# Scaling the prompt's attention probabilities in the product that transposes them

## The reference, cut to what matters

```
s = einsum('bqgjd,bsgd->bgjqs', q, k) + bias
p = masked_softmax(s, mask)          # exp(s - max) / sum
o = einsum('bgjqs,bsgd->bqgjd', p, v)
mix_n = g[0] * o_c + g[1] * o_s + g[2] * o_w      # g: sigmoid gates, one for each token, branch and head
```

## Time and profile before

| | us |
|---|---|
| median of 3 runs | 1063.69 (1063.34 to 1071.04) |
| the profiled execution | 1065.43 |
| its span, first to last instruction | 1063.7 |

### The profile page before, as it was taken

The page is one execution under the profiler, slowest core; times in us unless marked ns, Lnnn a source line. Parts: engine busy times, 40 slices in busy tenths (PEclk is TensorE's granted clock), DMA queues, the critical chain, the costliest instruction groups (busy, mean ns, idle before and its releaser), DMA issues.

```text
span 1063.7 us, 19859 instructions
## 1 busy us (share of the span) xinstructions
PE 921.4 (87%) x7903; PEld 824.2 (77%) x7903; DVE 517.3 (49%) x1116; ACT 374.3 (35%) x742; POOL 99.3 (9%) x164
## 2 busy tenths in 40 slices
PE   5865898899988758698888976999999999999994
PEld 5764687677877647355557966999999999999992
DVE  3610224642233564666664237667676676422325
ACT  4220234463532010155563136343443434222215
POOL 1001121334344000200000000000000000000000
PEclk9976898999999555558899998999999999999997
DMA  8256677757735000220003211232222222222212
GB/s 284 79 114 142 192 234 263 239 191 222 214 108 200 1 6 1 94 118 1 1 1 124 80 40 40 80 99 80 86 95 79 99 81 77 90 80 87 87 32 85
DMA packets 53135, 112.44 MB, mean 106 GB/s; under 512 B 6945, under 2 KB 30274, under 8 KB 52594
## 3 DMA queue, kind: packets, MB, share of 16 engines
q1 hardware_dynamic: 44616, 89.06, 25.3%
q0 software_dynamic: 6528, 17.83, 5.3%
q10 hardware_dynamic: 1898, 4.27, 2.5%
HBM read 102.92 MB, written 12.38 MB: 108 GB/s over the span
## 4 chain that ended last, share of the span: by engine, by line
PE 76%; DVE 9%; DMA 5%; ACT 4%; issue 3%; SPq 2%; ACTq 0%; POOLq 0%; POOL 0%; DVEq 0%
PE q L1667 28%; PE q L1665 26%; DMA arena<-in_pool 5%; PE q L2112 2%; PE q L2130 2%; PE q L2140 2%; PE q L1729 1%; PE q L2000 1%; PE q L2173 1%; PE q L2174 1%; PE q L2054 1%; PE q L1717 1%; PE q L1783 1%; PE q L1963 1%; DVE xt L1529 1%
## 5 line engine op out<-in xcount | busy, mean ns | idle before, releaser
L468 DVE TENSOR_TENSOR wring_r<-wring,whi_r 128x1024 fp32r<-128x1024 f32 (+1 forms) x101 | 120.5, 1193 | 366.9 <-ACT whi_r L465 366.7
L465 ACT ACTIVATE whi_r<-wring 128x1024 fp32r<-128x1024 f32 (+1 forms) x101 | 104.2, 1033 | 325.0 <-PE q L1667 314.3
L1667 PE MATMUL q<-xt_r,whi_r 128*128 128x288 f32 x552 | 167.7, 304 | 0.0
L1665 PE MATMUL q<-xt_r,whi_r 128*128 128x256 f32 x552 | 158.2, 287 | 0.0
L1665 PE MATMUL q<-arena_r,whi_r 128*128 128x256 f32 x440 | 138.0, 314 | 19.7 <-DVE xt_r L468 11.6
L1667 PE MATMUL q<-arena_r,whi_r 128*128 128x288 f32 x440 | 134.3, 305 | 0.0
L1667 PE MATMUL q<-arena_r,wring_r 128*128 128x288 f32 x440 | 133.5, 303 | 0.0
L1665 PE MATMUL q<-arena_r,wring_r 128*128 128x256 f32 x440 | 126.5, 287 | 0.0
L1665 PE MATMUL q<-mixt_r,whi_r 128*128 128x256 f32 x400 | 113.0, 282 | 10.5 <-DVE xt_r L468 10.5
L1667 PE MATMUL q<-mixt_r,whi_r 128*128 128x288 f32 x400 | 119.2, 298 | 0.0
L1665 PEld LDWEIGHTS q<-xt_r,whi_r 128*128 128x128 f32 x552 | 107.7, 195 | 0.0
(11 more groups left out here) (406 smaller groups left out, 1584.4 us busy)
## 6 DMA issues: line engine op xcount, KB each, us to landing
wring<-in_w_up SPq DMA_DIRECT2D x42, 512.0 KB, 3.3
wring<-in_w_in SPq DMA_DIRECT2D x27, 512.0 KB, 5.2
arena<-in_pool SPq DMA_DIRECT2D x64, 192.0 KB, 3.8
arena<-in_pool POOLq DMA_DIRECT2D x64, 192.0 KB, 4.2
wring<-in_w_down SPq DMA_DIRECT2D x24, 448.0 KB, 3.2
arena<-in_pool POOLq DMA_DIRECT2D x64, 64.0 KB, 2.5
arena<-in_pool SPq DMA_DIRECT2D x64, 64.0 KB, 2.2
wring<-in_w_out SPq DMA_DIRECT2D x8, 512.0 KB, 6.1
```

What stands on the lines that cost most here:

```text
L465: return eng.activation(out, src, ACT.Copy)
L468: return eng.tensor_tensor(out, src, hi.bitcast(F32), ALU.subtract)
L1665: pe.matmul(out[:, 0, 0:HALF], w, x[:, 0:HALF], start=(kk == 0 and n == 0), stop=(end and n == 2))
L1667: mm = pe.matmul(out[:, 1, 0:HALF + NS], w, x[:, HALF:NT], start=(kk == 0 and n == 0), stop=(end and n == 2))
```

## The change

`gated` no longer touches the probabilities. It writes the identity, scaled on each partition by the reciprocal of the sum and by the gate, to a new buffer of 3 slots x 2 heads x 128 columns in `dsc`. L1542 keeps its two instructions for each pair, and each is now 128 columns wide, whatever the width of the pair. `transposed` takes this scaled identity as the moving operand of an ordinary f32 product, where it had the plain identity in a transpose: out[key, query] = sum over p of pb[p, key] * diag[p, query]. The semaphores and their counts stay.

```
+        gated_one = dsc[:, 0:768].rearrange("p (s g c) -> p s g c", s=3, g=NG)
...
                 for g in range(NG):
-                    v, gate = pb[:, slot, g, 0:128 * i + 128], 104 + 24 * i + 8 * k + GQ * g + j
-                    dve.tensor_scalar(v, v, dens[:, 4 + slot, g:g + 1], gcol[:, gate:gate + 1],
+                    gate = 104 + 24 * i + 8 * k + GQ * g + j
+                    dve.tensor_scalar(gated_one[:, slot, g, :], ident, dens[:, 4 + slot, g:g + 1], gcol[:, gate:gate + 1],
                                       ALU.mult, ALU.mult).then_inc(np_p, 1)
...
                     for kk in range(m // 8 + 1):
-                        mm = pe.transpose(bank[4 + g][:, 128 * kk:128 * kk + 128],
-                                          pb[:, m % 3, g, 128 * kk:128 * kk + 128], ident)
+                        mm = pe.matmul(bank[4 + g][:, 128 * kk:128 * kk + 128],
+                                       pb[:, m % 3, g, 128 * kk:128 * kk + 128], gated_one[:, m % 3, g, :],
+                                       start=True, stop=True)
                     mm.then_inc(np_t, 1)
```

## The result

| | us |
|---|---|
| before, median of 4 runs | 1064.23 (1063.34 to 1071.04) |
| changed, median of 4 runs | 1080.40 (1079.21 to 1080.95) |
| changed / before | 1.0136, 95% interval 1.0093 to 1.0179 |
| the changed kernel's profiled execution, and its span | 1080.75, 1079.0 |

Slower by 16.2 us, 1.4%. The forecast was 1075.7 us, in a range of 1068 to 1081. Some kernels further on had one disturbed execution (1121, 1721 and 2194 us), which counts in the median that is given for them but not in the ratio.

A forecast was written before the change was run, and what follows sets the result against it. No engine was full; a loop of waits, TensorE holding the largest share, was taken to bound the prompt attention. 14.7 - 0.5 - 2.2 = +12.0 us on 1063.7 gave 1075.7 us, range 1068 to 1081.

The forecast's parts named there:

- The doubled instruction, 107 ns at the full clock: Line 2140: each product takes two instructions, so 160 more, each 107 ns at full clock, 0.215 us at half.
- Half of it on the path: Loop of two pairs: only every second transpose group stands in it, so about half of a group's extra time counts.
- The stretched chain, 14.7 us: Line 2140's pieces in the chain of waits, stretched: 6.0 at half clock, 6.6 at full, 2.1 in the last groups.
- The tail: Last two transpose groups, with no other work beside them: 0.76 us more each, 1.5 us for both.
- VectorE's pass, -0.5 us: Line 1542, now always 128 wide: 6.4 us less VectorE work, mostly hidden, 0.5 us of it gained.
- The clock, -2.2 us: Prompt attention: with ordinary products TensorE's clock rises a few us earlier than 480 us, taking back 2.2 us.
- the first (the clock pays it back): Prompt attention: products lift the clock early and return most of the cost; 1070 us, or 1067; chance 0.28.
- a hidden second instruction: Line 2140: the second instruction hides behind the weights' load, only VectorE's saving stays; 1063 us; chance 0.05.
- VectorE as the bound: Line 1542: VectorE's 6.4 us come back wholly; 1057 us with a hidden second instruction, about 1070 with doubled; chance 0.05.
- The second (all of it on the path): Line 2140: every stretched group delays a copy and shadows vanish, 20.6 - 0.5 us; 1084 us; chance 0.12.

The follow-up runs named there:

- the control: The kernel before, unchanged, measured and profiled once more: 1066.22 us median, ratio 1.0012, stage 112.3 us.
- short_scale: Against the kernel before: VectorE writes the scaled identity, but line 2140 stays a transpose with the plain identity, so probabilities are never scaled; 1065.22 us, ratio 0.9996.
- plain_product: Against the kernel before: line 2140 as an ordinary f32 product with the plain identity, VectorE still scaling the probabilities in place; 1079.5 us, ratio 1.0124.

## Why the prediction was right

It forecast +12.0 us. The stage grew by 11.8, and three measurements gave +16.2, +14.0 and +10.8. The time of the result, 1080.4 us, is another matter: it stands 0.6 us inside the range's upper end and above the forecast's own 1073 to 1079, because some 4 us came from outside the stage, of which the sum says nothing. That they left it in the range is luck. Step by step:

- *The doubled instruction, 107 ns at the full clock.* Right. L2141 has 320 instructions where L2140 had 160. A group of eight blocks was to take about 1.9 us and takes 1.98. The term was 0.09 us a group too small: the instruction's price was read from other lines and was right (two transposes in its place give 1.89), and the product form adds 0.09. The starts of the single instructions show how: at the full clock the second one of a group starts 0.21 us after the first where it is 0.16 with transposes, and each further one 112 ns after the last instead of 109. No row of before shows that. The lines that the price was read from bear it out in the trace of before: line 2173's two instructions start 0.215 us apart at a clock of 1.00, line 2000's, after the first, 0.213 us at 0.50. Line 2112's, 64 columns wide, start in pairs, 6 or 7 ns within a pair and 103 from one pair to the next, so that 16 of them take 1.03 us to the next group (546.96 to 547.99); it was rightly left aside. At the half clock the instruction costs 213 ns in the trace of after (215 in the sum), and the product form again adds, 0.10 us to the shortest group: the four of two blocks take 1.15 us to the next group (465.74 to 466.89), two transposes 0.62 (465.71 to 466.33 in the trace of before).
- *Half of it on the path.* Right in size, with another picture at the end. 8.2 us were forecast for two pairs, and 8.27 measured. The prediction noted that TensorE's own 4.0 us came near the loop's 4.1. In the trace of after they have met: TensorE has 0.1 us of waiting in two pairs. The kernel with three transposes shows the kink: two pairs go from 7.31 to 8.18 with the second and to 9.70 with the third, +0.9 and then +1.5, nearly the whole 2 x 8 x 0.107 = 1.7. The shadow hid only the first part of the growth here. The prediction's rule, half of the extra time, holds for the loop; tile 3 as a whole grew by 5.7 of 64 x 0.107 = 6.8 us, since its last groups have no such shadow.
- *The stretched chain, 14.7 us.* Split by tile, its pieces come to 1.9, 3.9, 3.6 and 5.3 us. Against the control, and with a third of a us given back for each us less at half, the tiles grew by 2.1, 3.2, 3.4 and 5.7. So the sum is right in its parts too, and not only in total.
- *The tail.* 0.76 us for each of the last two groups was forecast. The last output groups stand 3.76 us apart (570.62 and 574.38 in the chain), 2.92 before (557.19 and 560.10): 0.84, the same 0.09 too little.
- *VectorE's pass, -0.5 us.* Right: 0.5 to 0.7 us by short_scale, with 6 us less work, and 0.1 to 0.3 beside the doubled instruction.
- *The clock, -2.2 us.* An estimate of the author's and the least certain term, about right in size and in part by luck. By the clocks of the four tiles before, TensorE was at half for 17.6 + 18.7 + 7.0 = 43.3 us of the stage, after for 21.1 + 10.8 + 3.1 = 35.0. At 0.33 us each, the 8.3 us are worth 2.7 (3.3 at 0.4). So the price at an equal clock is 11.8 + 2.7 = 14.5 us, where the sum without the clock said 14.2. But the term was argued from one earlier rise, shortly before 480 us. Against the control, tile 1 has only 1.4 us less at half; 2.0 come from tile 0 and 3.9 from tile 2, of which the term says nothing. And the 34 us at half that the prediction counts from the earlier trace rows leave out the stage's first 9 us, up to 456.3, granted half as well; the 0.81 of the earlier trace rows over 115 us makes it 44.

Of the rivals, the first (the clock pays it back) was at work, but with about a fifth of the cost (2.7 of 14.5 us, by the estimate above) and not with most of it. The third and fourth (a hidden second instruction; VectorE as the bound) are excluded by plain_product and short_scale. The second (all of it on the path) is true only of a third transpose in the widest pairs, 6.8 of 6.8 us.

It took the clock to rise sooner with ordinary products in place of the transposes. That was the author's estimate, and the runs bear it out at most in tile 0 (0.57 with products, 0.50 with two transposes). Over the stage two transposes for each block gave 0.86 and 0.84 where the changed kernel had 0.86, and three gave 0.89, the highest of all, with all of these instructions in the transpose form. In tile 3 of that kernel 24 of a pair's 44 instructions are transposes, and the granted clock was 1.00 throughout. In the kernel before, 60 transposes in a row ran at 1.00 for 7.3 us.

## What to carry to other kernels

Ask first what the pass costs where it stands, and then what it becomes where it goes. Here VectorE's pass was waited for 1.1 us in the whole stage, and 6 us less of it were worth 0.5 to 0.7 us (short_scale). In the product the same scaling made two instructions of each transpose, 320 on line 2141 for 160 on line 2140, and these 160 more cost 12 us (plain_product).

Read the price of an instruction from a line with the same shape of weights: line 2173, 128 x 128, gave 107 ns, and 112 were measured, while line 2112 with 64 columns shows 64 ns (1.03 us for 16). Then ask how much of it a loop of waits covers, and look at how near the engine's own time is to the loop's. Here they met at 8.27 us for two pairs with 0.1 us of waiting left; a second transpose for each block added 0.9 us to two pairs, a third 1.5. When two kernels differ by one per cent, compare the length of the stage that was changed, with its clock, and not the whole time alone: the stage grew by 11.6 to 12.1 us over all pairs of profiles here, while the differences of whole times ran from 10.8 to 16.2 us.

## What the hardware showed unasked

- The clock is part of the result. With the same number and length of TensorE instructions, the fp32r form had a stage clock of 0.75 and 0.70 where the transposes had 0.81, and the stage was 5.6 and 10.3 us longer than the control's, 16.7 and 30.6 us more at half clock. With more work on TensorE in the same loop it stood higher (0.81 with one transpose for each block, 0.86 and 0.84 with two, 0.89 with three), which gave back part of that work's cost: by the estimate of 0.33 us for each us at half, 2.7 us of the doubled products' (first profiles of before, 0.81, and of the changed kernel, 0.86). Why it stood lower with one fp32r product than with one transpose of the same length stays open.
- An fp32r product of 128 columns with 128 x 128 weights took about as long here as the f32 transpose of that size, 1.04 us for eight to the next group where the transposes took 1.02, while the f32 products of eight blocks took 1.98. That type gave no gain over the transpose in either of its two runs.
- One kernel's stage start wandered from 444.1 to 447.6 us between two profiles, and the kernels that share that beginning ranged up to 454.2, with all of it before the changed code.
